# Row places handed out later, rows moved ahead of the residual sums and into the scan, in a hybrid SSD, attention and PEER block

## The reference

```python
def block(xb):                              # 128 tokens
    q = (xb @ w_q).reshape(tb, PEER_HEADS, 2, PEER_HALF)
    sc = einsum('thjd,hjnd->thjn', q, sub_keys)
    s_half, i_half = lax.top_k(sc, 16)
    ...                                     # 16x16 candidates, top 16 of them, softmax g
    u_sel = u[idx]                          # 8 heads x 16 rows of 1024 for each token
    v_sel = v[idx]
    h = gelu(einsum('td,thkd->thk', xb, u_sel))
    return einsum('thk,thkd->td', g * h, v_sel)
```

## Time and profile before

| | us |
|---|---|
| median of 3 runs | 1438.3 (1437.46 to 1440.38) |
| the profiled execution | 1438.13 |
| its span, first to last instruction | 1436.2 |
| TensorE, VectorE, ScalarE, GpSimd busy | 1379.3, 1098.2, 411.8, 618.8 |
| moved by DMA | 467.69 MB, 326 GB/s in the mean |
| 512 gathers on GpSimd's queue | 268.47 MB of it |

### The profile page before, as it was taken

One profiled execution on the slowest core, in us unless ns is written; L12 is line 12 of the kernel. 1 busy time (PEld: TensorE's weight loads), 2 busy tenths in 40 slices (PEclk: granted clock), 3 DMA queues, 4 the chain that ended last, 5 costly groups with the idle time before them and its releaser, 6 DMA issues.

```text
span 1436.2 us, 16310 instructions
## 1 busy us (share of the span) xinstructions
PE 1379.3 (96%) x5402; PEld 936.5 (65%) x5402; DVE 1098.2 (76%) x2545; ACT 411.8 (29%) x1147; POOL 618.8 (43%) x516
## 2 busy tenths in 40 slices
PE   7999999998999999999999999999999999999996
PEld 5556648566478888888888889985444444444442
DVE  4535445798799999999888899997867767775666
ACT  2443522443331111112666676672000000000000
POOL 0000000641755532532355677665477655654541
PEclk9999999999999999999999999999999999999998
DMA  7233334983999998897799999999999999999997
GB/s 296 99 117 132 118 121 180 346 293 129 381 387 386 387 340 308 334 358 269 272 377 377 368 372 388 384 375 391 338 409 409 409 409 409 409 410 409 409 410 309
DMA packets 121331, 467.69 MB, mean 326 GB/s; under 512 B 13728, under 2 KB 14112, under 8 KB 114720
## 3 DMA queue, kind: packets, MB, share of 16 engines
q0 software_dynamic: 73728, 268.47, 48.7%
q1 hardware_dynamic: 47520, 198.19, 35.9%
HBM read 462.67 MB, written 3.93 MB: 325 GB/s over the span
## 4 chain that ended last, share of the span: by engine, by line
PE 41%; DMA 29%; DVE 18%; issue 5%; POOL 4%; ACT 3%; DVEq 0%; SPq 0%; ACTq 0%
PE BANKS L897 14%; DMA BIG<-u,IDX 8%; DMA BIG<-v,IDX 8%; PE BANKS L922 8%; PE BANKS L699 8%; PE BANKS L691 7%; DMA UV<-v,IDX 7%; DVE X L1546 5%; DMA UV<-u,IDX 4%; POOL UV L1591 4%; DVE UV L1541 2%; DVE BIG L1541 1%; PE BANKS L880 1%; DVE BIG L1280 1%; DVE NMX L1481 1%
## 5 line engine op out<-in xcount | busy, mean ns | idle before, releaser
L1591 POOL DMA_INDIRECT UV<-u,IDX x147 | 184.4, 1254 | 418.0 <-DVE IDX L1427 260.2
L1591 POOL DMA_INDIRECT UV<-v,IDX x165 | 201.4, 1220 | 154.5 <-DVE UV L1541 74.7
L1546 DVE SCALAR_TENSOR_TENSOR X<-UV,HG,X 128x1024 f32<-128x1024 f32 x165 | 211.7, 1283 | 39.1 <-DMA UV<-v,IDX 35.4
L897 PE MATMUL BANKS<-T 128*128 128x256 f32 x1024 | 229.2, 379 | 1.6 <-DMA T<-u_t 1.6
L922 PE MATMUL BANKS<-T,BIG 128*128 128x512 f32 x512 | 225.3, 593 | 1.4 <-DVE BIG L1562 1.1
L922 PE MATMUL BANKS<-Y,BIG 128*128 128x512 f32 x512 | 225.1, 592 | 0.0
L897 PE MATMUL BANKS<-T,Y 128*128 128x256 f32 x992 | 221.9, 379 | 0.0
L1541 DVE SCALAR_TENSOR_TENSOR UV<-UV,Y 128x1024 f32<-128x1024 f32 x147 | 178.9, 1224 | 52.8 <-DMA UV<-u,IDX 51.2
L897 PEld LDWEIGHTS BANKS<-T 128*128 128x128 f32 x1024 | 192.0, 190 | 26.6 <-DMA T<-u_t 2.0
L897 PEld LDWEIGHTS BANKS<-T,Y 128*128 128x128 f32 x992 | 186.0, 190 | 24.0
L922 PEld LDWEIGHTS BANKS<-T,BIG 128*128 128x128 f32 x512 | 97.0, 190 | 124.1 <-issue 120.7
(11 more groups left out here) (278 smaller groups left out, 1219.0 us busy)
## 6 DMA issues: line engine op xcount, KB each, us to landing
T<-u_t SPq DMA_DIRECT2D x64, 512.0 KB
T<-v SPq DMA_DIRECT2D x64, 512.0 KB
Y<-v SPq DMA_DIRECT2D x64, 512.0 KB
Y<-u_t SPq DMA_DIRECT2D x62, 512.0 KB
BIG<-w_in SPq DMA_DIRECT2D x23, 1024.0 KB
BIG<-w_q SPq DMA_DIRECT2D x16, 1024.0 KB
BIG<-w_out SPq DMA_DIRECT2D x8, 1024.0 KB
UV<-v,IDX POOLq DMA_INDIRECT x165
```

What stands on the lines that cost most here:

```text
L897: last = nc.tensor.matmul(PS[(i + 2) % 4][:, 0:HT], ub[:, c, :], T8[:, 1, c, :], start=(c == 0), stop=(c == KC - 1))
L1546: stt(xb, row, HG[:, n % 2, i % UNIT:i % UNIT + 1], xb, ALU.mult, ALU.add).then_inc(used, 1)
L1591: pool.indirect_dma_start(row_place(s), None, u if kind == "ru" else v, bass.IndirectOffsetOnAxis(IDX[:, b, c:c + 1], 0)).then_inc(row_in[ ...
```

## The change

It has three parts, all of them order.

1. `in_use` replaces the constant: ST may be used from the 27th row instead of the 24th, QT from the 37th instead of the 33rd, SEG from the 45th (before the 39th), both of PP from the 44th (before the 39th). K and XBC stay. A place then opens later in the row order; until then the rows take places of the ring.
2. The scan's step S1 loses its two products, line 1329, to a step M of its own. In the first half M follows S1 directly, as before. For chunk 2, three of the eight rows that followed S1 now stand ahead of M; for chunk 3, `qs q1` and two rows do.
3. After the second half's attention the residual sums get more rows ahead: 5 instead of 2 before the first, 6 instead of 4 before the second, 7 instead of 5 before the third. That is 7 rows more ahead of everything that follows, with the same number of rows at each later place; the remainder between `gm` of the last group and choice 5 shrinks from 8, 4 and 2 rows to 5, 2 and 1.

```diff
--- before.py
+++ after.py
@@ -115,8 +115,8 @@
     for i in range(5, 8):
         o += many("x", i, i + 1) + many("cv", i - 1, i)
     o += on("acs", 0) + many("cv", 7, 8) + on("hl ea", 0)
-    o += on("z", 0) + on("z", 1) + on("S1", 0) + on("q", 0) + on("q", 1) + on("S2", 0) + on("k", 0) + on("S3", 0)
-    o += on("S1", 1) + on("qs q1", 0) + on("k", 1) + on("S2", 1) + on("q2", 0) + on("ks k1", 0) + on("v", 0) + on("S3", 1)
+    o += on("z", 0) + on("z", 1) + on("S1 M", 0) + on("q", 0) + on("q", 1) + on("S2", 0) + on("k", 0) + on("S3", 0)
+    o += on("S1 M", 1) + on("qs q1", 0) + on("k", 1) + on("S2", 1) + on("q2", 0) + on("ks k1", 0) + on("v", 0) + on("S3", 1)
     o += on("k2", 0) + on("v", 1) + many("qt", 0, 4)
 
     def attention(first, end, after, between):
@@ -155,8 +155,8 @@
         return many("r", b * PH + 2 * q, b * PH + 2 * q + 2) + on("y", n)
 
     o += many("cv", 14, 16) + many("W", 0, 4) + many("K", 0, 2) + on("ks k1", 1) + many("W", 4, 8) + many("K", 2, 4)
-    o += pick(0) + on("z", 2) + on("k2", 1) + on("S1", 2) + on("z", 3) + many("qt", 4, 6) + rows(8)
-    o += on("q", 2) + on("S2", 2) + on("q", 3) + on("S3", 2) + rows(5) + on("S1", 3) + on("qs q1", 1) + rows(2)
+    o += pick(0) + on("z", 2) + on("k2", 1) + on("S1", 2) + on("z", 3) + many("qt", 4, 6) + rows(3) + on("M", 2) + rows(5)
+    o += on("q", 2) + on("S2", 2) + on("q", 3) + on("S3", 2) + rows(5) + on("S1", 3) + on("qs q1", 1) + rows(2) + on("M", 3)
     o += on("v", 2) + on("q2", 1) + on("v", 3) + rows(2) + on("S2", 3) + many("qt", 6, 8) + on("S3", 3) + rows(2)
     at_start = many("W", 8, 9) + rows(2)
     first, second, keys = pick(1)
@@ -165,7 +165,7 @@
     for i in range(8, 16):
         after[i] = many("W", i + 1, min(i + 2, 16)) + (between[i] if i in between else rows({8: 4, 12: 1, 13: 3, 14: 3, 15: 0}[i]))
     after[15] = on("T", 2)
-    after[15] += on("N n2", 3) + rows(2) + on("R0", 2) + on("T", 3) + rows(4) + on("R0", 3) + rows(5) + on("R1 Q", 2)
+    after[15] += on("N n2", 3) + rows(5) + on("R0", 2) + on("T", 3) + rows(6) + on("R0", 3) + rows(7) + on("R1 Q", 2)
     after[15] += rows(4) + on("F", 2) + rows(1) + on("R1 Q", 3) + on("U", 2) + many("K", 4, 6) + on("F", 3) + many("K", 6, 8) + on("U", 3) + rows(7)
     o += attention(8, 16, after, at_start)
     o += many("W", 16, 20) + many("K", 8, 10) + pick(2) + rows(7) + many("W", 20, 24) + many("K", 10, 12)
@@ -419,8 +419,10 @@
 
 
 
+            in_use = {"K": RING + 3, "ST": RING + 3, "QT": RING + 4, "SEG": RING + 6, "PP": RING + 5}
+
             def opened(step, name, at, guard, end):
-                first = RING + at // DM if name == "XBC" else rows_until(step) + RING + 3 * (name == "K") + 1
+                first = RING + at // DM if name == "XBC" else rows_until(step) + in_use.get(name, RING) + 1
                 return first_of[name] + at, first, guard, end
             tile = lambda name, at: ("gl", min(FIRSTJ, (first_of[name] + at) // HT - 1))
             early = [
@@ -1323,6 +1325,8 @@
                 if b < NB - 1:
                     dve.wait_ge(dt_act, 6)
                     tt(hd3(XDTE), hd3(XDT), bc(DTE[:, b, :], 2, HD), ALU.mult).then_inc(xdt_ready, 1)
+
+            def ssd_weighted(b):
                 for g in range(NG):
                     dve.wait_ge(seg_exp, NG * b + g + 1)
                     m = SEG[:, g, :].rearrange("p (h n) -> p h n", n=P)
@@ -1460,6 +1464,8 @@
                     tt(DTE[:, :, :], ACS[:, :, NH:2 * NH], ACS[:, :, 0:NH], ALU.subtract).then_inc(dt_step, 1)
                 elif step == "S1":
                     ssd_first(i)
+                elif step == "M":
+                    ssd_weighted(i)
                 elif step == "S2":
                     ssd_second(i)
                 elif step == "S3":
```

## The result

Twenty executions of each kernel, taken together, gave a median of 1435.23 us for the kernel before and 1440.99 us for the changed one, a ratio of 1.0039 with a 95% interval of 1.0021 to 1.0058. Two executions of the changed kernel, 1456.82 and 1457.13 us, lie over 1.5% above its fastest and are left out of the ratio. The change costs 0.4%; the forecast was a gain of 0.15%, with a range of 1432.5 to 1440.0 us. The profiled execution took 1448.78 us, its span is 1446.7. That is well above the median, so the numbers of this first profile are set beside a second one of the same kernel further down.

A forecast was written before the change was run, and what follows sets the result against it. The rows, slowed by full DMA engines in the last stage, were taken to end last. Lateness 4.6, gain 6.8 and 0 for the rest gave -2.2 on the 1436.2 us span; plus 1.9 around it, 1435.9 us, range 1432.5 to 1440.0.

The forecast's parts named there:

- The views of the end: End of the kernel: rows finish 7.3 us after the last matmuls, so at most about 7.1 us can be won.
- Places and map weighting: Later-opening places and rows inside the scan: each taken as 0 us, bounds -1 to +1.3 and -0.9 to +0.5.
- The third choice: VectorE after the residual sums: would start at 413.3 us, 6.9 us late, waiting for the 62nd row's data.
- the first rival: Gathers ahead of the third choice: data keep up, choice at about 409, lateness 2.5 us, time 1433.8 us; chance 0.30.
- The step that failed: From third choice to last stage: VectorE stays 6.9 us late, less 2.3 of waiting, shifting the last stage's start by 4.6.
- compute alone: Rows ahead of the residual sums: without data waits, third sum 2.8 us late, fourth sum and TensorE's second half 2.3.
- the 2.3 us in hand: VectorE's first wait for the transposed choice, at about 680 us: would absorb 2.3 us of its lateness.
- the 7.0 us booked for seven rows: Last stage: seven fewer gathers save 9.0 us, restart loses 2.0; 6.8 taken as won, bounds 5.5 and 7.1.
- The restart at the sixth choice: Last stage, gathers of unit 5: GpSimd waits some 18.5 us instead of 12.65, costing 2.0 us.
- The slower one: Last seven gathers ahead of the third choice take 3.8 us each, choice 15 us late, time 1444 us; chance 0.10.
- Its deciding point: Third choice: if it starts later than 415.5 us the change loses, by over 0.2% from 418.4.
- Rival (c): Last stage: gathers' restart costs 5 us, not 2, and rows still end last, time 1438.7 us; chance 0.15.

The follow-up runs named there:

- group 1: Against the kernel before: changed kernel unaltered 1.0034, without the seven moved rows 1.0000, with 5, 6, 5 rows 1.0032; the kernel before with the seven rows alone 1.0036.
- group 5: The kernel before with 2, 4, 8 rows ahead of the residual sums, 0.9997, beside it with 5, 4, 5 rows, 0.9995.
- 5, 6, 7 with nothing behind: Changed kernel without the seven rows between the second half's last transposes and the third choice, against the kernel before: 1.0082.
- group 3: Against the kernel before: changed kernel without rows behind the transposes 1.0082, 5, 4, 5 rows alone 0.9972, last TensorE products left out of changed kernel 1.0042, of kernel before 1.0002.
- shortened changed kernel: Changed kernel with the fourth token block's products left out for four of the last v tiles, against the kernel before: 1.0042.

## Why the prediction was wrong

**The views of the end were read rightly.** The rows ended last before, 7.3 us behind TensorE. With TensorE's last products left out of that kernel the time stays (1.0002), and with three rows moved the two ends meet, 1.2 us apart.

**Places and map weighting** were costed at 0; measured 1.0000 (0.9983 to 1.0018) for both without the rows. Right, within that interval.

**The third choice** was forecast at 413.3, from the data of the 62nd row; measured 415.37, 414.14 and 413.6 in the three profiles. The mechanism is right, and the view of the queues agrees. Packets of the gathers from 362 to 409 us without and with the moved rows, beside the 3324 of the earlier trace rows:

```profile
q0 software_dynamic: 3453, 12.60, 67.6%
```

```profile
q0 software_dynamic: 3569, 13.01, 69.6%
```

At 144 packets a row, seven more rows wanted brought 0.8 rows more, which is inside the scatter: two profiles of the kernel before have 3324 and 3667, 2.4 rows apart. From 248 to 413 us 9085 and 9237 packets moved, 63.1 and 64.1 rows. The Trainium skill's price of a GpSimd DMA (DMA: Bandwidth & Descriptors, Anatomy of one DMA), by which every row would have been in time, is not what a full queue gives; the measurement decides, and the first rival falls.

**The step that failed is the next one**: "it stays 6.9 late until it meets its own 2.3 us of waiting: 4.6 us late from there on". That term, 4.6, measured 12.3 us. Three things were wrong in it, and a fourth in what was set against it.

First, the size. On one chip the third choice was 8.9 us late, not 6.9: the data were already missing ahead of the third sum, where the prediction had put compute alone.

Second, the 2.3 us in hand. That was one wait in one profile: 2.32 and 6.77 in two profiles of the kernel before, none in the changed kernel without the rows. It comes with TensorE's own lateness, such as its stops for tiles of u, and nothing of VectorE's lateness was seen to vanish in it.

Third, lateness was taken as constant up to the last stage. It grew from 8.9 to 12.3, since rows wait for data again (2.53 us at 607.59), and since TensorE stands for VectorE at about 705 to 710 (4.49 us in this profile of the changed kernel, 4.75 and 7.33 with five rows), after which its granted clock is down for a while. The other two profiles of the changed kernel don't have this stop; there TensorE itself was later by some 12 us since the copies that the last section shows.

Fourth, the gain. The last stage gave back more than the 7.0 us booked for seven rows, 11.9, and it was of no use: the lateness ate it at the rows' end, and TensorE's end does not profit from it. The traffic shows both. From 362 to 467 us, where the DMA engines were at a share near 1.00, a row that is *asked for* earlier isn't moved earlier: 7512 packets without and 7559 with the moved rows, 0.3 rows. They are made up from 467 to 690, the stretch with room:

```profile
q0 software_dynamic: 10699, 38.96, 45.7%
```

```profile
q0 software_dynamic: 11693, 42.55, 50.2%
```

That is 994 packets, 6.9 rows. It holds beyond this pair: from 362 to 690, two profiles of the kernel before and the changed kernel without the rows have 18098 to 18211 packets, the three of the changed kernel 18909 to 19367. Behind 690 much of it is lost again. Around TensorE's stop the DMA engines are not full (columns as in the earlier trace rows), without and with the rows:

```profile
705.00:720.00 15.00, 14.38 (x83) 12.79 (x82) 10.66 (x19) 7.44 (x24) 6.48 (x8) 1.00 0.98 361
```

```profile
705.00:720.00 15.00, 10.51 (x48) 9.14 (x47) 14.76 (x28) 5.02 (x17) 8.71 (x7) 0.77 0.66 216
```

From 362 to 990 us, again without and with the rows, both queues:

```profile
q0 software_dynamic: 39491, 143.82, 59.6%
q1 hardware_dynamic: 21766, 85.67, 35.8%
```

```profile
q0 software_dynamic: 39884, 145.25, 60.2%
q1 hardware_dynamic: 21058, 82.50, 34.7%
```

393 packets, 2.7 rows, were won by 990 us, and 3.17 MB of tiles, six of 0.524 MB, had not come yet, because TensorE was behind. The rows' end stayed where it was, where the prediction had it 2.2 us sooner. TensorE's end, which had 7.3 us in hand by the earlier trace rows and 8.4 in group 1, moved by 11.8. With 12.3 in place of 4.6 the prediction's own sum, its gain held to the 8.4 us that TensorE had in hand, gives +3.9 us, where the spans differ by 3.4. The form of the sum was right; the lateness in it was not.

**The restart at the sixth choice** was well read: GpSimd waits 17.50 and 18.35 us for it in the changed kernel, against the forecast of 18.5, and 11.51 without the rows. The third choice is a restart of the same kind: GpSimd waits 13.58 us there without the rows and 13.62 with them, but issues again at 431.14 instead of 422.27. That was not costed at all.

**The rivals.** The slower one, with the data as its mechanism, was nearest and had 0.10; its rate of 3.8 us a row, which puts the choice 15 us late, was not measured. Its deciding point, a third choice later than 415.5, was wrong: 414.14 was enough, by the second and third point above. Rival (c) was near in size, 1438.7, for a wrong reason: the last stage gave back more, not less.

**What stays open.** The path of the loss was followed in one pair of profiles, which shows 3.4 of the 4.9 us between the medians. The rows alone and the kernel with five rows (5, 6, 5) were profiled in executions that lost nothing, so where their usual executions lose 0.3% isn't seen. Whether the place of the rows matters at an equal number: 2, 4, 8 equals 5, 4, 5 in group 5, while 5, 6, 7 with nothing behind costs 0.8% in group 3, from seven executions. And whether five rows really cost more ahead of the sums (0.3%) than behind them (0.06%): the intervals overlap, from 1.0016 to 1.0022, and the groups are different ones.

## What to carry to other kernels

Where transfers fill the DMA engines, putting their consumers earlier in the order of an engine moves no data in that stretch (0.3 rows of seven here); it makes that engine wait, and all that stands behind it. The bytes are made up where there is room (here 467 to 690, share 0.89), but the lateness stays. So follow the lateness through every later wait before setting a gain against it. And where two chains end within 7 us of each other, carry both through the sum: a gain on the one is capped by the other, and a lateness that both share is paid in full once the cap is used. Dose such a change: three rows gained up to 0.28%, in two groups of three, where seven cost 0.34%. Take slack from more than one profile, and see how far the profiled execution lies from the median before reading a loss in it.

## What the runs showed of the hardware

**Copies 5.0 us apart.** In the first profile of the changed kernel, and again in the third, ScalarE waited for TensorE's key products, which by TensorE's records had been through for some time. In the first one TensorE itself also stood 3.85 us for a tile of the keys, at 410.31. ScalarE there:

```profile
404.63 0.60 ACT L1127 ACTIVATE BIG<-BANKS 128x512 f32<-128x512 f32 x1
409.62 0.60 ACT L1127 ACTIVATE BIG<-BANKS 128x512 f32<-128x512 f32 x1 [4.39 <-remote]
...
414.62 0.60 ACT L1127 ACTIVATE BIG<-BANKS 128x512 f32<-128x512 f32 x1 [2.95 <-remote]
...
419.67 0.60 ACT L1127 ACTIVATE BIG<-BANKS 128x512 f32<-128x512 f32 x1 [4.45 <-remote]
```

They come 4.99, 5.00 and 5.05 us apart, where the second profile has 1.5 to 2.0 us. In the third the steps are 4.96 and 7.08. It moved TensorE's second half from 408.57 to 421.44 and 419.96, some 12 us, which is more than the whole effect of the change. The cause is not known. Such rows of steps were seen only where the third sum was late, and there in two of the three profiles of the unaltered change, in none of the kernel before (the shortened changed kernel of group 3 has a single step of 5.03 us, between copies of query products); the changed kernel's executions also spread over 27 us (1429.95 to 1457.13), those of the kernel before over 11. It may be a part of the loss that no sum from a profile could have given.

**The clock after a stop.** Windows of the second profile (columns as in the earlier trace rows): the first takes in most of a stop of 5.21 us for the normed tokens (its end at 399.06), the third a stop of 4.49 us for the one-hots (its end at 710.10):

```profile
394.00:402.00 8.00, 2.94 (x14) 2.94 (x15) 6.68 (x14) 3.76 (x10) 6.17 (x7) 0.70 1.03 416
402.00:410.00 8.00, 6.57 (x43) 6.12 (x43) 3.95 (x5) 6.52 (x19) 6.47 (x6) 0.87 1.02 409
703.00:713.00 10.00, 5.51 (x25) 4.79 (x24) 9.86 (x17) 1.86 (x6) 3.83 (x3) 0.74 0.45 150
```

The granted clock of 0.70, 0.87 and 0.74 is a mean over stretches at 2.4 GHz and at 1.2. Eight matmul records of the one-hot transposes took 2.07 us at the lower one, 1.05 at the higher. So a stop of TensorE of this length cost more than its length here: each such group of eight records at the lower clock took 1.02 us more.
